# The last strip of each gated feed-forward, transposed and rounded by token tile

## The reference

```python
D_MODEL = 1024; SEQ = 256; DEPTH = 2; D_FF = 2816

def swiglu(x, w_gate, w_up, w_down):
    return (jax.nn.silu(x @ w_gate) * (x @ w_up)) @ w_down

for l in range(DEPTH):
    f = swiglu(rmsnorm(x, ffn1_pre_g[l]), ffn1_w_gate[l], ffn1_w_up[l], ffn1_w_down[l])
    x = x + 0.5 * rmsnorm(f, ffn1_post_g[l])
    m = token_mixing(rmsnorm(x, mix_pre_g[l]), ...)
    x = x + rmsnorm(m, mix_post_g[l])
    f = swiglu(rmsnorm(x, ffn2_pre_g[l]), ffn2_w_gate[l], ffn2_w_up[l], ffn2_w_down[l])
    x = x + 0.5 * rmsnorm(f, ffn2_post_g[l])
```

## Time and profile before

| | |
|---|---|
| three runs | 1938.1, 1948.16, 1946.51 us; median 1946.51 |
| profiled execution | 1938.25 us, span 1936.6 us, mean granted clock 0.997 |
| TensorE busy | 1907.7 us (99%) |
| VectorE, ScalarE, GpSimd busy | 1068.6, 1039.1 and 1582.7 us |
| transposes by VectorE (line 1839) | 960, 343.8 us |

### The profile page before, as it was taken

How to read it: one execution, slowest core, us unless ns; L and a number is a source line. 1 busy time by engine, 2 the same in 40 slices (tenths; PEclk the granted TensorE clock), 3 DMA queues, 4 the chain that set the end, 5 groups by cost and what they waited for, 6 DMA issues and landing times.

```text
span 1936.6 us, 26834 instructions
## 1 busy us (share of the span) xinstructions
PE 1907.7 (99%) x9394; PEld 1546.9 (80%) x9394; DVE 1068.6 (55%) x2662; ACT 1039.1 (54%) x1762; POOL 1582.7 (82%) x1160
## 2 busy tenths in 40 slices
PE   9999999999999999999999999999999999999999
PEld 7888777888788877788887877778888777778887
DVE  6868445444644744554445677446444577654552
ACT  6445666444644466654466454655456554555543
POOL 7988776988798877598879787779887968788986
PEclk9999999999999999999999999999999999999999
DMA  6765434666665553467565343456667433336664
GB/s 240 240 212 176 162 120 151 191 192 194 205 233 192 183 163 120 136 216 258 194 212 196 120 142 120 142 175 215 234 194 253 149 123 131 120 135 202 193 193 137
DMA packets 98209, 346.87 MB, mean 179 GB/s; under 512 B 13436, under 2 KB 14108, under 8 KB 97820
## 3 DMA queue, kind: packets, MB, share of 16 engines
q1 hardware_dynamic: 97372, 344.03, 54.2%
q10 hardware_dynamic: 704, 1.14, 0.2%
HBM read 344.08 MB, written 1.05 MB: 178 GB/s over the span
## 4 chain that ended last, share of the span: by engine, by line
PE 89%; POOL 4%; ACT 3%; DVE 3%; issue 1%; DMA 0%; SPq 0%; POOLq 0%; ACTq 0%; DVEq 0%
PE psum L585 27%; PE psum L587 26%; PE psum L586 26%; POOL lo L558 4%; PE psum L755 1%; PE psum L656 1%; DVE psum L1839 1%; PE psum L778 1%; PE psum L765 1%; PE psum L988 1%; PE psum L745 1%; ACT hi L1281 1%; ACT big L1646 1%; PE psum L801 0%; PE psum L842 0%
## 5 line engine op out<-in xcount | busy, mean ns | idle before, releaser
L558 POOL TENSOR_TENSOR lo<-raw,hi 128x256 fp32r<-128x256 f32 (+2 forms) x1156 | 1582.5, 1393 | 339.7 <-ACT hi L1281 310.8
L1281 ACT ACTIVATE hi<-raw 128x1024 fp32r<-128x1024 f32 (+1 forms) x616 | 642.9, 1054 | 502.2 <-PE psum L587 466.9
L585 PE MATMUL psum<-hi,h_hi 128*128 128x512 f32 (+1 forms) x1632 | 648.6, 397 | 7.9 <-POOL lo L558 7.7
L587 PE MATMUL psum<-hi,h_lo 128*128 128x512 f32 (+1 forms) x1632 | 635.4, 389 | 0.0
L586 PE MATMUL psum<-lo,h_hi 128*128 128x512 f32 (+1 forms) x1632 | 634.3, 389 | 0.0
L585 PEld LDWEIGHTS psum<-hi,h_hi 128*128 128x128 f32 x1632 | 307.8, 189 | 76.1 <-issue 8.6
L587 PEld LDWEIGHTS psum<-hi,h_lo 128*128 128x128 f32 x1632 | 306.9, 188 | 64.4
L586 PEld LDWEIGHTS psum<-lo,h_hi 128*128 128x128 f32 x1632 | 307.7, 189 | 59.5
L1839 DVE STREAM_TRANSPOSE psum<-big 32x128 f32<-32x128 f32 (+1 forms) x960 | 343.8, 358 | 14.2
L585 PE MATMUL psum<-hi,y_hi 128*128 128x512 f32 x832 | 328.9, 395 | 6.0 <-DVE big L2300 4.0
L587 PE MATMUL psum<-hi,y_lo 128*128 128x512 f32 x832 | 324.8, 390 | 0.0
(11 more groups left out here) (263 smaller groups left out, 1317.0 us busy)
## 6 DMA issues: line engine op xcount, KB each, us to landing
raw<-in_stream SPq DMA_DIRECT2D x608, 512.0 KB, 4.2
big<-in_w SPq DMA_DIRECT2D x14, 512.0 KB, 5.8
big<-in_post SPq DMA_DIRECT2D x6, 512.0 KB, 4.5
special<-in_b_merge SPq DMA_DIRECT2D x2, 1536.0 KB, 8.8
raw<-in_stream SPq DMA_DIRECT2D x8, 296.0 KB, 5.3
memkv<-in_mem SPq DMA_DIRECT2D x2, 1024.0 KB, 7.5
big<-in_band SPq DMA_DIRECT2D x2, 768.0 KB, 6.1
x<-in_x SPq DMA_DIRECT2D x2, 512.0 KB, 4.9
```

What stands on the lines that cost most here:

```text
L558: t = pool.tensor_tensor(M.lo[:, slot, w], M.raw[:, slot, w], f32(M.hi[:, slot_hi, w]), ALU.subtract)
L585: pe.matmul(out, lhs_hi, rhs_hi, start=start, stop=False)
L587: return pe.matmul(out, lhs_lo, rhs_hi, start=False, stop=stop)
L1281: act.activation(M.hi[:, slot_hi, used], M.raw[:, slot, used], ACT.Copy).then_inc(sem["hi"], 1)
```

## The change

The last strip of each gated feed-forward no longer goes through `turn` and `low`. `last_by_tile` takes its place, on VectorE and on ScalarE. On VectorE, for each token tile in turn: 16 transposes of 32x64 (both feature tiles, one token tile) into a PSUM bank of the tile's own, a signal, a wait for ScalarE's rounding of that half, and the subtraction for that half. So the low part of tile 0 comes before the transposes of tile 1. ScalarE rounds two halves of 128x256. TensorE waits for the half of tile 0 before the third feature tile of token tile 0, and for the half of tile 1 before the third of token tile 1. The semaphores' counts follow (`parts_before`). Nothing else is moved: the table load, the weight pieces and the squares stand behind the rounding of the second half on ScalarE. The plain feed-forwards stay as they are.

```diff
-def halves_before(s):
+def parts_before(s):
 
     gated = L * 2 * FFN_STRIPS
-    return s if s < gated else gated + 2 * (s - gated)
+    return s + s // FFN_STRIPS if s < gated else gated + 2 * L + 2 * (s - gated)
...
-                if m == 0 and i in ylo:
-                    pe.wait_ge(sem["ylo"], ylo[i])
+                if (m, i) in ylo:
+                    pe.wait_ge(sem["ylo"], ylo[m, i])
...
-        last_rows(c, order, y_hi, y_lo, (4, 6), turn_next, {0: done - 1, 2: done})
+        ylo = {(0, 0): done - 2, (0, 2): done - 1, (1, 2): done} if gated else {(0, 0): done - 1, (0, 2): done}
+        last_rows(c, order, y_hi, y_lo, (4, 6), turn_next, ylo)
...
+        def last_by_tile(c, s):
+            act.wait_ge(sem["used"], c)
+            for m in range(MT):
+                kt, toks = (s - n0) % 2 * kts, slice(m * P, m * P + P)
+                act.wait_ge(sem["turned"], s + s // FFN_STRIPS + m + 1)
+                act.activation(y_hi[:, kt:kt + 2, toks], by_k(psum[:, 2 + m, 0:S]), ACT.Copy).then_inc(sem["yhi"], 1)
...
         if gated:
-            turn(c, n0 + strips - 1)
+            last_by_tile(c, n0 + strips - 1)
             exp_and_ln()
...
+        def last_by_tile(s):
+
+            dve.wait_ge(sem["prod"], s + 1)
+            for m in range(MT):
+                turned = by_k(psum[:, 2 + m, 0:S])
+                src = prod_s[:, m, :].rearrange("p (k c) -> p k c", k=2)
+                for b in range(4):
+                    for a in range(4):
+                        t = dve.transpose(turned[32 * b:32 * b + 32, :, 32 * a:32 * a + 32],
+                                          src[32 * a:32 * a + 32, :, 32 * b:32 * b + 32])
+                t.then_inc(sem["turned"], 1)
+                kt, toks = (s - n0) % 2 * kts, slice(m * P, m * P + P)
+                dve.wait_ge(sem["yhi"], parts_before(s) + m + 1)
+                dve.tensor_tensor(y_lo[:, kt:kt + 2, toks], turned, f32(y_hi[:, kt:kt + 2, toks]),
+                                  ALU.subtract).then_inc(sem["ylo"], 1)
...
             product(s)
+            if gated and s == n0 + strips - 1:
+                last_by_tile(s)
+                break
             turn(s)
             if once:
                 once(s - n0)
-        low(n0 + strips - 1)
+        else:
+            low(n0 + strips - 1)
```

More of the change, by code:

```diff
@@ L208, in flat, with by_k @@
     return a.rearrange("p a b -> p (a b)")
+def by_k(a):
+    return a.rearrange("p (k t) -> p k t", k=2)
 def tiles(a):
@@ L719, in down @@
         def down(c, s):
-            pe.wait_ge(sem["ylo"], halves_before(s + 1))
+            pe.wait_ge(sem["ylo"], parts_before(s + 1))
             for i in range(kts):
@@ L734, in feed_forward @@
         order = [(strips - s) % 2 * kts + i for s in ((2, 1) if gated else (1,)) for i in range(kts)]
-        done = halves_before(n0 + strips)
-        last_rows(c, order, y_hi, y_lo, (4, 6), turn_next, {0: done - 1, 2: done})
+        done = parts_before(n0 + strips)
+        ylo = {(0, 0): done - 2, (0, 2): done - 1, (1, 2): done} if gated else {(0, 0): done - 1, (0, 2): done}
+        last_rows(c, order, y_hi, y_lo, (4, 6), turn_next, ylo)
         return c + 4
@@ L1386, in turn @@
                 kt = (s - n0) % 2 * kts + 2 * g
-                act.wait_ge(sem["turned"], s + 1)
+                act.wait_ge(sem["turned"], s + min(s // FFN_STRIPS, 2 * L) + 1)
                 act.activation(flat(y_hi[:, kt:kt + 2, :]), psum[:, bank + g, :], ACT.Copy).then_inc(sem["yhi"], 1)
+        def last_by_tile(c, s):
[4 more added lines that the diff above has]
+                act.activation(y_hi[:, kt:kt + 2, toks], by_k(psum[:, 2 + m, 0:S]), ACT.Copy).then_inc(sem["yhi"], 1)
         project(c, n0)
@@ L1846, in low @@
                 kt = (s - n0) % 2 * kts + 2 * g
-                dve.wait_ge(sem["yhi"], halves_before(s) + g + 1)
+                dve.wait_ge(sem["yhi"], parts_before(s) + g + 1)
                 dve.tensor_tensor(flat(y_lo[:, kt:kt + 2, :]), psum[:, bank + g, :],
```

## The result

| | before | after |
|---|---|---|
| median of eight runs | 1939.07 us | 1954.36 us |
| lowest to highest | 1937.95 to 1948.16 | 1952.87 to 1964.33 |
| profiled execution, span | 1938.25, 1936.6 | 1953.92, 1952.3 |
| mean granted clock | 0.997 | 0.993 |

The ratio is 1.0078, 95% interval [1.0062, 1.0095]: the change costs 15.3 us by the medians and 15.7 by the profiled executions, where 14.1 were forecast. Some executions of a kernel last 7 to 10 us longer than its others (two of the eight of before, one of the eight after), and two of the three of before that were shown ahead were such. With more runs before lies at 1939, so the base of the forecast, 1942.4, was 3.3 us too high, and the added part 1.2 too small: the two errors partly cancel, and that the forecast of 1956.5 lies only 2.1 us from 1954.36 is to that extent luck.

A forecast was written before the change was run, and what follows sets the result against it. TensorE, busy 99% of 1936.6 us, was taken to bound the kernel. Four stages x 2.4 = 9.6 us plus 4.5 us for the clock gave 14.1 us on 1942.4: 1956.5 us, range 1942 to 1966.

The forecast's parts named there:

- (a): VectorE's last-strip transposes: 32 of 32x64 replace 16 of 32x128, 4.3 us a half, 8.6 us where 5.4 were.
- B: Rival: short transposes are cheap, 2.7 us a half; squares 0.36 us late a stage, 1944 us; chance 0.13.
- C: Rival: short transposes cost as much as long ones, 5.36 us a half; 23 us more, 1965 us; chance 0.09.
- (c): First half's order: low part ends at 182.42, TensorE needs it at 183.37; the stall goes with 0.9 us to spare.
- A: Rival: only the stall goes, the squares aren't late; 3.0 us less, 1939.4 us; chance 0.05.
- (d): Second half on VectorE: low part done by 187.68, second tile's matmuls want it at 188.8, on time by 1.1 us.
- (e): ScalarE's queue behind the second rounding: squares 2.4 to 2.5 us late, TensorE stands some 3.2 us before the transposes of x.
- (f): Entry into the next stage moves as a block by 2.4 us, nothing swallows it; 4 stages give 9.6 us.
- D: Rival: a DMA or GpSimd wait swallows the delay later; 0 to 5 us, 1942 to 1947 us; chance 0.05.
- (g): Clock falls behind TensorE's 3 us holes in three stages of four, 1.5 us each: 4.5 us, bounds 0 and 6.

The follow-up runs named there:

- e_order: Changed kernel with ScalarE's table load and the rounding of piece c+4 moved in front of the second half's rounding: 1939.9 us, ratio 1.0001 against before.
- e_table: Changed kernel with ScalarE's table load alone moved in front of the second half's rounding: 1943.45 us, ratio 1.0020 against before.
- e_fill: Changed kernel with 12 extra matmuls per gated feed-forward in TensorE's hole before the transposes of x: 1949.43 us, ratio 1.0045 against before.
- e_both: Changed kernel with both tiles' transposes in front of the first low part on VectorE: 1952.9 us, ratio 1.0064 against before.

## Why the prediction was right

The forecast case happened, and each step can be held against a row.

- (a) A transpose of 32x64 lasts 0.256 us and 16 take 4.30, forecast 4.3. One row for all 128 of them (group by form: busy us, mean ns):

```profile
L1864 DVE STREAM_TRANSPOSE psum<-big 32x64 f32<-32x64 f32 x128 | 32.8, 256 | 1.9
```

The step is (4.30 - 0.26) / 15 = 0.269 us: the line through the two forms in the earlier trace rows holds one step further down, with 0.2 us that don't depend on the size. That closes rivals B and C. It also closes the 0.22 us, an estimate, that the Trainium skill's figure for the fixed cost gave (VectorE: DVE Perf Modes, "The TRN2 errata"); the rows of before already spoke against it, since the same estimate gives 0.29 and 0.42 us for the two longer forms, which step by 0.336 and 0.469. The advice in that section, larger instructions instead of many small ones, is borne out: half the elements cost 80% of the time.
- (c) The first low part was early, the stall went. Case A had that much right.
- (d) The second low part ended at 187.31 on the axis of after; nothing waited for it.
- (e) The squares were forecast 2.4 to 2.5 us late and came 2.36 to 2.40 late, by the way described: `e_order` takes ScalarE's tail out of it and the delay is within 0.02; `e_table` takes half of the tail and it is 0.96.
- (f) The hole before the transposes of x was forecast at 3.2 us and came to 3.04. The delay was not swallowed (case D). The entry into the next stage moved with it, in the four stages alike.
- (g) The clock fell in four places of four, forecast three, at 1.07 to 1.50 us each, forecast 1.5: 5.2 us for 4.5. This is the mis-sized term, and it lay within its bounds of 0 and 6. That it is paid on top, `e_fill` shows. What the Trainium skill says of it (TensorE: Matmul & The Clock Gate, "What's actually happening"), that activity releases a throttled default, fits both kernels: hole empty, 0.95; hole filled, 1.00. The four falls don't follow from the length of the hole alone: the "two holes together" of the earlier trace rows are one of 2.85 us and one of 0.31, and the single one, nearly as long as the forecast's 3 us, had left the clock at 1.00.

Not forecast were the 0.4 us in the second mixer and the 0.9 in the second block. The first appears in the four other kernels with 32 short transposes (0.33 to 0.36 us at the same place) and not in the two with 16 long ones; its cause isn't tested. In the second block the granted clock fell three times after the change and twice before. Which holes there meet a fall differs from kernel to kernel with nothing changed near them, and the six kernels of the experiments take from 0.2 us less to 1.7 us more than before in that block, so the 0.9 us say nothing about the edit.

What decided was to follow what is queued behind the moved instruction, on its own engine. By the wait that the change removes alone, it would have been a gain of 3 us.

## What to carry to other kernels

An engine that works in order passes a delay on to everything behind it: when a signal is split in two, look at what stands behind the wait for the second half, and put work that doesn't need it between the halves. Splitting instructions that carry a fixed part (here 0.2 us of 0.34) to let a first half out earlier makes the second half late by that part times their number (here 3.2 us, and 1 us more for the first half's rounding and subtraction that stand between). Splitting only the cheap steps behind them, the rounding and the subtraction, took 0.46 of the 0.76 us of the stall and made no stage longer. A hole of 3 us in TensorE's work can cost more than its length: at the four places of this kernel it cost another 1.1 to 1.5 us, since the clock fell.

## What the runs showed of the hardware that had not been expected

**The same small VectorE operation took 0.4 to 18.4 us.** The profiled execution of `e_table` lasted 1951.99 us, where the median is 1943.45. Its timeline of VectorE early in the first feed-forward, and TensorE's:

```profile
52.44 18.41 DVE L2432 CAST small<-small 128x3 f32<-128x3 int32 x1
70.89 0.50 DVE L2434 TENSOR_SCALAR extra<-small 128x8 f32<-128x8 f32 x3
```

```profile
72.95 0.79 PE L590 MATMUL psum<-hi,h_hi 128*128 128x512 f32 x1 [5.97 <-DVE big L1841]
```

In the kernel before the same cast took 2.42 us:

```profile
52.03 2.42 DVE L2398 CAST small<-small 128x3 f32<-128x3 int32 x1
```

and the three small operations behind it 7.03. A conversion of three columns took 18.4 us in one execution and 2.4 in another (0.41 after the change, 1.85 to 2.34 in the other five), and in `e_table` the next strip's product came so late that TensorE stood for 6.0 us and started again at the lower clock. Why it takes so long isn't shown. In a comparison of a few tenths of a per cent it counts.

**How long a hole is didn't settle whether the clock fell behind it.** At the ends of the gated feed-forwards it looks like a matter of length: the clock fell behind four of four holes of 3.04 us (after) and four of four of 2.8 (`e_both`), behind none of four of 1.63 (`e_table`), none of 0.7 (`e_order`), and none of 3.04 us filled with matmuls. But in the second block, where the code is the same in all kernels, one hole of 2.85 us left the clock at 1.00 before the change, and in `e_order`, and met a fall after it:

```profile
1510.34 0.47 PE L585 MATMUL psum<-hi,h_hi 128*128 128x512 f32 x1 [2.85 <-POOL lo L558]
1510.65 0.40 PE L586 MATMUL psum<-lo,h_hi 128*128 128x512 f32 x1
```

```profile
1525.20 0.76 PE L590 MATMUL psum<-hi,h_hi 128*128 128x512 f32 x1 [2.85 <-POOL lo L563]
1525.76 0.63 PE L591 MATMUL psum<-lo,h_hi 128*128 128x512 f32 x1
```

Holes of 2.0 us met a fall in one case and not in the other. So these runs give no length from which a fall is sure, and what else decides isn't tested. The eight transposes of x behind the holes of 3.04 us didn't prevent the fall.
